# Gathering the tokens of an expert in one-pass products, and turning the SwiGLU rows 128 at a time

## The reference, cut to what matters

```python
x = x + gt1 * mix
h = rmsnorm(x, norm_ffn) * (1.0 + sc2) + sh2
# one group of 4 by argmax, its top 2 of 8 experts, softmax weights: comb
for grp in range(4):
    hg  = einsum('nd,edf->enf', h, w_exp_gate[grp])     # 8 experts, 2048 -> 512
    hu  = einsum('nd,edf->enf', h, w_exp_up[grp])
    hid = silu(hg) * hu * wgt.T[:, :, None]
    out = out + einsum('enf,efd->nd', hid, w_exp_down[grp])
```

## Time and profile before

| | us |
|---|---|
| median of 3 runs | 1876.94 |
| the profiled execution | 1875.18 |
| its span | 1873.5 |
| PE busy, weight loads busy | 1771.7, 1267.9 |
| DVE, ACT, POOL busy | 714.0, 471.0, 212.7 |

### The profile page before, as it was taken

One profiled execution on the slowest core, in us unless ns is written; L12 is line 12 of the kernel. 1 busy time (PEld: TensorE's weight loads), 2 busy tenths in 40 slices (PEclk: granted clock), 3 DMA queues, 4 the chain that ended last, 5 costly groups with the idle time before them and its releaser, 6 DMA issues.

```text
span 1873.5 us, 37855 instructions
## 1 busy us (share of the span) xinstructions
PE 1771.7 (95%) x16527; PEld 1267.9 (68%) x16527; DVE 714.0 (38%) x1523; ACT 471.0 (25%) x842; POOL 212.7 (11%) x295
## 2 busy tenths in 40 slices
PE   5689999999988989999899999999999999999997
PEld 2168779988856666899666656666566665666656
DVE  1145564455673554643222333222322223222234
ACT  3044333444621211344211111111111111111114
POOL 1000000021038780333000000000000000000000
PEclk8889999999999999899999999999999999999997
DMA  9989884674388779342699999999999999999992
GB/s 365 419 304 335 299 309 135 202 254 152 135 310 349 297 301 372 109 146 91 281 431 428 434 431 432 432 430 434 429 434 430 432 432 430 435 428 434 431 432 78
DMA packets 111124, 629.71 MB, mean 336 GB/s; under 512 B 8932, under 2 KB 76956, under 8 KB 81823
## 3 DMA queue, kind: packets, MB, share of 16 engines
q1 hardware_dynamic: 105150, 608.45, 80.1%
q0 software_dynamic: 5120, 17.44, 2.8%
q10 hardware_dynamic: 754, 2.33, 0.4%
HBM read 618.65 MB, written 9.56 MB: 335 GB/s over the span
## 4 chain that ended last, share of the span: by engine, by line
PE 43%; DMA 13%; DVE 1%; issue 0%; ACT 0%; POOL 0%; POOLq 0%; DVEq 0%; ACTq 0%
PE pb L2712 18%; DMA ring<-in_w_exp_up 13%; PE pb L2691 7%; PE pb L2725 6%; PE pb L2701 2%; PE pb L2702 2%; PE pb L2069 2%; PE pb L2070 2%; PE pb L2071 1%; PE pb L2734 1%; PE pb L2607 0%; PE pb L2744 0%; PE pb L2741 0%; PE pb L2614 0%; PE pb L2742 0%
## 5 line engine op out<-in xcount | busy, mean ns | idle before, releaser
L2712 PE MATMUL pb<-ring,pj 128*64 128x256 f32 x4096 | 466.0, 381 | 5.8 <-DMA ring<-in_w_exp_up 5.8
L2712 PEld LDWEIGHTS pb<-ring,pj 128*64 128x64 f32 x4096 | 285.9, 137 | 170.6 <-DMA ring<-in_w_exp_up 19.9
L2069 PE MATMUL pb<-ht_parts,ring_parts 128*128 128x264 f32 x1056 | 309.2, 293 | 7.1 <-DVE ring_parts L1324 6.2
L2070 PE MATMUL pb<-ring_parts 128*128 128x264 f32 x1056 | 301.9, 286 | 0.0
L2071 PE MATMUL pb<-ring_parts 128*128 128x264 f32 x1056 | 301.4, 285 | 0.0
L2725 PE MATMUL pb<-ring,pj 128*64 128x512 f32 x1024 | 226.0, 594 | 0.0
L2069 PEld LDWEIGHTS pb<-ht_parts,ring_parts 128*128 128x128 f32 x1056 | 201.6, 191 | 24.1 <-issue 16.0
L1864 DVE TENSOR_TENSOR pj_parts<-pb,pj_parts 64x512 fp32r<-64x512 f32 x128 | 88.2, 689 | 311.3 <-ACT pj_parts L1186 309.3
L2070 PEld LDWEIGHTS pb<-ring_parts 128*128 128x128 f32 x1056 | 201.8, 191 | 0.0
L2071 PEld LDWEIGHTS pb<-ring_parts 128*128 128x128 f32 x1056 | 200.7, 190 | 0.0
L1324 DVE TENSOR_TENSOR ring_parts<-ring,ring_parts 128x2048 fp32r<-128x2048 f32 x50 | 114.6, 2291 | 173.6 <-ACT ring_parts L790 173.5
(11 more groups left out here) (470 smaller groups left out, 1962.4 us busy)
## 6 DMA issues: line engine op xcount, KB each, us to landing
ring<-in_w_exp_gate SPq DMA_DIRECT2D x32, 4096.0 KB, 17.7
ring<-in_w_exp_up SPq DMA_DIRECT2D x32, 4096.0 KB, 15.5
ring<-in_w_exp_down SPq DMA_DIRECT2D x32, 4096.0 KB, 17.1
ring<-in_w_ada SPq DMA_DIRECT2D x32, 2048.0 KB, 15.2
ring<-in_w_in SPq DMA_DIRECT2D x24, 2048.0 KB, 9.3
pj<-in_w_ada SPq DMA_DIRECT2D x32, 1024.0 KB, 7.8
ring<-in_w_ada_final SPq DMA_DIRECT2D x16, 2048.0 KB, 13.0
ring<-in_w_out SPq DMA_DIRECT2D x8, 2048.0 KB, 8.5
```

The lines of the kernel that those rows point to most:

```text
L2069: pe.matmul(out, hi[:, k, :], ht_lo[:, k, :], start=(k == 0), stop=False)
L2070: pe.matmul(out, lo[:, k, :], ht_hi[:, k, :], start=False, stop=False)
L2712: last = pe.matmul(pb[bank][SLOT * h:SLOT * h + SLOT, e * 256:(e + 1) * 256], xg[:, k, SLOT * e:SLOT * e + SLOT], w[:, k, h * 256:(h + 1) ...
```

## The change

Each token block is written once in two parts: `h_hi`, the scaled token rounded to float32r, and `h_lo`, the remainder. The gather multiplies both with `disp`, now also float32r (0 and 1). The two parts take 4 MB together: `h_lo` takes the place of `h_tok`, and `h_hi` lies in five pieces in memory of three tensors that are free by then (`lm`, `ct`, `ada_row`) and in the free end of `ht`. ACT writes the five pieces of `h_hi`, two ahead of the first exponential, two behind it, one behind the second; POOL scales `h_tok` in place and subtracts `h_hi`, piece by piece (10 instructions). The first gather waits for two remainders, the third for all five. `moe_turn` becomes 4 transposes of all 128 rows, and ACT takes each of them out in two copies.

```diff
+        h_lo = pj_r[:, at[0]:at[0] + TC * D].rearrange("p (c k r) -> p c k r", c=TC, r=P)
         h_tok = room(TC * D).rearrange("p (c k r) -> p c k r", c=TC, r=P)
+        H_HI = [[(range(0, 8), lm_r[:]), (range(8, 12), ct_r[:]), (range(12, KD), ada_r[:])],
+                [(range(0, 8), ht_r[:, D + P:D + P + 1024]), (range(8, KD), ht_r[:, D + P + 1024:2 * D + P])]]
+        H_ORDER = [(0, 0), (1, 0), (0, 1), (0, 2), (1, 1)]
...
+            pool.wait_ge(*once("rs_mid"))
+            pool.wait_ge(S("h2t_evac"), KD)
+            for i, (c, part) in enumerate(H_ORDER):
+                ks, mem = H_HI[c][part]
+                at = slice(ks[0], ks[-1] + 1)
+                pool.wait_ge(S("h_norm"), i + 1)
+                pool.tensor_scalar(h_tok[:, c, at, :], h_tok[:, c, at, :], ms_tok[:, c:c + 1], None, ALU.mult)                    .then_inc(S("h_scaled"), 1)
+                pool.wait_ge(S("h_scaled"), i + 1)
+                pool.tensor_tensor(h_lo[:, c, at, :], h_tok[:, c, at, :], mem.bitcast(F32).rearrange("p (k r) -> p k r", r=P),
+                                   ALU.subtract).then_inc(S("h_low_out"), 1)
...
-            tokens_out(0)
+            act.wait_ge(*once("rs_mid"))
+            act.wait_ge(S("h2t_evac"), KD)
+            for c, part in H_ORDER[0:2]:
+                tokens_out(c, part)
             act.wait_ge(*once("rt_d1"))
             act.activation(g_exp, g_exp, ACT.Exp).then_inc(once("rt_e1")[0], 1)
+            for c, part in H_ORDER[2:4]:
+                tokens_out(c, part)
             act.wait_ge(*once("rt_d2"))
             act.activation(e2, e2, ACT.Exp).then_inc(once("rt_e2")[0], 1)
-            tokens_out(1)
+            tokens_out(*H_ORDER[4])
...
-                    act.copy(hid_t[:, e], pb[6][:, e * 256:(e + 1) * 256].rearrange("p (c s) -> p c s", s=SLOT))\
-                        .then_inc(S("m_ht"), 1)
+                    turned = pb[6][0:SLOT, :].rearrange("p (c h s) -> p h c s", h=2, s=SLOT)
+                    act.copy(hid_t[0:SLOT, e], turned[:, 0])
+                    act.copy(hid_t[SLOT:P, e], turned[:, 1]).then_inc(S("m_ht"), 1)
...
                 for j in range(4):
+                    k = 4 * b + j
                     for c in range(TC):
-                        last = pe.matmul(pb[bank][:, j * P:(j + 1) * P], h_tok[:, c, 4 * b + j, :], disp[:, c, :],
-                                         start=(c == 0), stop=(c == TC - 1))
+                        pe.matmul(pb[bank][:, j * P:(j + 1) * P], h_lo[:, c, k, :], disp_r[:, c, :], start=(c == 0), stop=False)
+                        last = pe.matmul(pb[bank][:, j * P:(j + 1) * P], h_hi(c, k), disp_r[:, c, :], start=False, stop=(c == TC - 1))
...
                 for c in range(4):
-                    for h in range(2):
-                        r = slice(SLOT * h, SLOT * h + SLOT)
-                        last = pe.matmul(pb[6][r, e * 256 + c * SLOT:e * 256 + (c + 1) * SLOT], sg_in_rows[r, e, c, :],
-                                         ident[r, r], start=True, stop=True)
+                    last = pe.transpose(pb[6][0:SLOT, c * P:(c + 1) * P], sg_in_rows[:, e, c, :], ident[:])
...
                     pe.wait_ge(S("sh_evac"), 4)
+                    pe.wait_ge(S("h_low_out"), 5)
                     moe_gather(2, FIRST_BANKS[2])
...
-                    pe.wait_ge(S("h_norm"), TC)
+                    pe.wait_ge(S("h_low_out"), 2)
                     moe_gather(0, FIRST_BANKS[0])
```

More of the change, by code:

```diff
@@ L103, in sb @@
             return ctx.enter_context(nc.sbuf_tensor(name, [rows, cols], dt))
-        sizes = (("ring", (MOE_SLOTS - 1) * RING + KD * NT), ("ht", KD * NT), ("g2", 1024), ("pj", NTILE * NT))
+        sizes = (("ring", (MOE_SLOTS - 1) * RING + KD * NT), ("ht", KD * NT), ("g2", 1024), ("pj", NTILE * NT),
+                 ("lm", 8 * P), ("ct", KD * CPAD), ("ada_row", BANK))
         with ExitStack() as parts:
-            ring_r, ht_r, g2_r, pj_r = (parts.enter_context(nc.sbuf_tensor(f"{name}_parts", [P, cols], F32R))
+            ring_r, ht_r, g2_r, pj_r, lm_r, ct_r, ada_r = (parts.enter_context(nc.sbuf_tensor(f"{name}_parts", [P, cols], F32R))
                                   for name, cols in sizes)
-        ring, ht_flat, g2, pj_flat = (sb(name, cols) for name, cols in sizes)
+        ring, ht_flat, g2, pj_flat, lm_flat, ct_flat, ada_row = (sb(name, cols) for name, cols in sizes)
         ta = ring[:, MIX_SLOTS * RING:MOE_SLOTS * RING]
@@ L122, in hymba_layer @@
         bones = sb("bones", P)
-        ct = sb("ct", KD * CPAD)[:].rearrange("p (k n) -> p k n", n=CPAD)
-        lm = sb("lm", 8 * P)[:].rearrange("p (l n) -> p l n", n=P)
+        ct = ct_flat[:].rearrange("p (k n) -> p k n", n=CPAD)
+        lm = lm_flat[:].rearrange("p (l n) -> p l n", n=P)
         mstrict = sb("mstrict", P)
@@ L132, in hymba_layer @@
         om_ka = sb("om_ka", 8)
-        ada_row = sb("ada_row", BANK)
         rstd = sb("rstd", NT)[:]
@@ L240, in hymba_layer, with h_hi @@
         most_f, most = room(1), room(1).bitcast(I32)
+        h_lo = pj_r[:, at[0]:at[0] + TC * D].rearrange("p (c k r) -> p c k r", c=TC, r=P)
         h_tok = room(TC * D).rearrange("p (c k r) -> p c k r", c=TC, r=P)
+        H_HI = [[(range(0, 8), lm_r[:]), (range(8, 12), ct_r[:]), (range(12, KD), ada_r[:])],
+                [(range(0, 8), ht_r[:, D + P:D + P + 1024]), (range(8, KD), ht_r[:, D + P + 1024:2 * D + P])]]
+        H_ORDER = [(0, 0), (1, 0), (0, 1), (0, 2), (1, 1)]
+        def h_hi(c, k):
+            at, = [mem[:, (k - ks[0]) * P:(k - ks[0] + 1) * P] for ks, mem in H_HI[c] if k in ks]
+            return at
         xg = room(KD * P).rearrange("p (k s) -> p k s", s=P)
@@ L247, in hymba_layer @@
         hid_t = room(FF).rearrange("p (e c s) -> p e c s", e=2, s=SLOT)
+        disp_r = pj_r[:, at[0]:at[0] + TC * P].rearrange("p (c s) -> p c s", c=TC)
         disp = room(TC * P).rearrange("p (c s) -> p c s", c=TC)
@@ L1132, in _, with tokens_out @@
             mid_out(KD - 1)
[L1134 to L1138, removed]
-            tokens_out(0)
+            def tokens_out(c, part):
+                ks, mem = H_HI[c][part]
+                act.activation(mem.rearrange("p (k r) -> p k r", r=P), h_tok[:, c, ks[0]:ks[-1] + 1, :], ACT.Identity,
+                               scale=ms_tok[:, c:c + 1]).then_inc(S("h_norm"), 1)
+            act.wait_ge(*once("rs_mid"))
+            act.wait_ge(S("h2t_evac"), KD)
+            for c, part in H_ORDER[0:2]:
+                tokens_out(c, part)
             act.wait_ge(*once("rt_d1"))
             act.activation(g_exp, g_exp, ACT.Exp).then_inc(once("rt_e1")[0], 1)
+            for c, part in H_ORDER[2:4]:
+                tokens_out(c, part)
             act.wait_ge(*once("rt_d2"))
             act.activation(e2, e2, ACT.Exp).then_inc(once("rt_e2")[0], 1)
-            tokens_out(1)
+            tokens_out(*H_ORDER[4])
             def sh_out(b):
@@ L1831, in moe_dispatch @@
                     for c in range(TC):
-                        last = dve.tensor_scalar(disp[:, c, q * SLOT:(q + 1) * SLOT], slot_no[:, 0, :],
+                        last = dve.tensor_scalar(disp_r[:, c, q * SLOT:(q + 1) * SLOT], slot_no[:, 0, :],
                                                  slots[:, c, bass.ds(t * 2 + q, 1)], None, ALU.is_equal)
@@ L2740, in moe_places @@
                 for c in range(TC):
-                    pe.matmul(pb[6][:, 0:2], disp[:, c, :], comb[:, c, bass.ds(i * 2, 2)], start=(c == 0), stop=False)
+                    pe.matmul(pb[6][:, 0:2], disp_r[:, c, :].bitcast(F32), comb[:, c, bass.ds(i * 2, 2)], start=(c == 0), stop=False)
                 pe.matmul(pb[6][:, 0:2], own_slot, comb[0:NS, TC, bass.ds(i * 2, 2)], start=False, stop=True)
                 for c in range(TC):
-                    last = pe.transpose(pb[7][:, c * P:(c + 1) * P], disp[:, c, :], ident[:])
+                    last = pe.transpose(pb[7][:, c * P:(c + 1) * P], disp_r[:, c, :].bitcast(F32), ident[:])
                 last.then_inc(S("m_wt"), 1)
```

## The result

The changed kernel takes 1889.97 us (median of 4 runs, 1886.39 to 1892.24) against 1877.63 us for the kernel before beside it: ratio 1.006, 95% interval 1.0045 to 1.0075. Worked out from the ratio that is +11.3 us, 8.4 to 14.1; the two medians themselves lie 12.3 us apart. The forecast was 1883 us. With 1889.97 us the result also lies beyond the 1886.3 us from which the prediction calls a time "slower", to which it gave a chance of 0.36.

The account below looks back on a forecast made before the run. DMA bounds the expert loop, so only head and tail count: head +8.0 - 0.4, tail -0.4 - 0.6, +6.6 us on 1875.18 is 1881.8; with 1.8 us to the runs' median, 1883. Range about 1873 to 1893.

Parts of the forecast that it names:

- The loop hides it: Expert loop: DMA sets the pair's 58.3 us, so a shorter PE part, busy some 56.5, changes nothing.
- Gather, 111 ns a product, set by the weight load: Gather parts: loading 128 stationary columns sets the pace, so a part takes 1.78 us in place of 1.88.
- -0.4 us in the tail: Tail after the last "up 1": four gather parts, each 0.1 us shorter.
- Turn, -0.6 us: Tail: 4 transposes take 0.43 to 0.5 us in place of 1.09; hidden in the loop.
- The lock of POOL and DVE, 7 to 10, taken as 8: Head, routing chain: POOL's instructions hold off DVE's two-input ones, so `routed` comes 7 to 10 us late.
- Nothing later is delayed in its own right: Head behind routing: PE, ACT and SP only wait behind `routed`; DMA's empty stretch grows by as much.
- -0.4 in the head from the gathers: Head, first gathers: four parts, each 0.1 us shorter.
- Rival A: Routing chain: POOL holds DVE with whole instructions, +11.5 to +15 in the head, 1887 to 1891 us; chance 0.22.
- B: Head: small DVE instructions slip by or scaling doesn't lock, 0 to 5 us, 1875.5 to 1880.5; chance 0.15.
- C: Gathers: 128 columns, not the weight load, pace the product; about 1876 us, without delay 1868; chance 0.10.
- D: Gathers: one-pass product takes 236 ns at 128 columns, PE becomes the bound, about 1990 us; chance 0.08.

Follow-up runs that it names:

- five-fold low products: Changed kernel with the first low product of each tile issued five times in place of once; 1982.36 us, ratio 1.0552.
- without POOL: Changed kernel with POOL's ten instructions left out, the low product multiplying the rounded part again; 1880.59 us, ratio 1.0024.
- pace measurement: Changed kernel with seven series of 24 float32r products, of varied stationary and moving columns, ahead of the counting; 1900.74 us, series included.
- layout alone: Kernel before, with only lm, ct and ada_row allocated as in the changed kernel; 1877.46 us, ratio 1.001.
- late POOL: Changed kernel, but POOL starts its third piece only when the first dispatch is done; 1886.93 us, ratio 1.0062.
- fillers: Changed kernel plus float32 products on the identity in PE's idle time, 28 ahead of the counting and 15 ahead of the first gather; 1880.4 us, ratio 1.0023.
- DVE remainder: Changed kernel with the remainder made by DVE in eight instructions of 512 columns, POOL idle; 1882.02 us, ratio 1.0026.
- DVE remainder, fillers: Changed kernel with DVE making the remainder, plus 3 float32 products ahead of the counting and 7 ahead of the first gather; 1879.03 us, ratio 1.0013.
- all cuts: Kernel before with its float32 gather, the new turn, 3 + 7 filler products, and the last pair's gather parts cut to one product; 1872.97 us, ratio 0.9966.
- peel: Kernel before with only the last pair written out, its four gather parts being one product of 64 columns each; 1872.25 us, ratio 0.9975.
- turn alone: Kernel before with only moe_turn changed to 4 transposes and two ACT copies; 1874.99 us, ratio 0.9988.

## Why the prediction was right and wrong

The measured +11.3 us lies inside the range, and the sign is right; the forecast of +6.6 was 4.7 us low. By its own steps:

- **The loop hides it: right.** 58.28 us a pair, PE busy 56.48 (forecast 56.5). The five-fold low products confirm 1.8 us of slack.
- **Gather, 111 ns a product, set by the weight load: right in the pace** (112 ns by itself, 108 in place in the loop, 64 moving columns no quicker than 128). The -0.4 us in the tail was not seen: the two gathers of 32 gave 0.05 us each (3.77 to 3.72; 3.57 beside the same turn to 3.52). I had set a computed 1.78 us against a measured 1.88; in the chain the new gather goes at 3.72 / 32 = 116 ns.
- **Turn, -0.6 us: mis-sized**, 0.85 us with the gather behind it. The tail came out at -0.9 for a forecast -1.0, by two errors that met. The 106 ns of a transpose were a slip: sixteen starts have fifteen intervals, so the earlier trace rows give (1.95 - 0.275) / 15 = 112 ns, and four in the chain took 0.44 to 0.46 us, within the stated 0.43 to 0.5.
- **The lock of POOL and DVE, 7 to 10, taken as 8: right as a mechanism, mis-sized at 6.2 us.** Without POOL it is 0.05 us (10.71 against 10.66). The single holds were right: a subtraction was priced at 2.2 us and adds 2.02 and 2.10, a scaling was priced at 0.86 us (1024 columns) and 0.43 (512) and adds 0.87 and 0.45. What failed is the window between holds. It was taken as 0.2 to 0.3 us, since POOL's scaling was priced like a copy, with the whole sequence at 14 us. The scaling of 1024 columns took 2.86 us, and from the first POOL instruction to the end of the last it is 21.8 us (901.69 to 923.47). (Spans on POOL are rough, but the start of the next instruction says the same: 2.94 us behind the scaling, 2.32 behind the subtraction.) After that first stretch of a scaling DVE ran freely: at 903.51, in the midst of it, L1806 takes 0.18 us. So routing was done after five holds, 6.3 us, and not after the 8 us that were reckoned from nearly all of them. Subtracting holds for its whole length. The Trainium skill ("SBUF — State Buffer", section "SBUF: two separate sides") has the lock held for the whole instruction; the trace agrees for the subtraction and not for the scaling.
- **"Nothing later is delayed in its own right": this step failed.** It holds the other 6.6 us of the head (12.74 less 6.18). Not all of them are the lock's, since the head of the kernel without POOL is still 3.3 us longer than before. Because POOL was still at work when routing was done, the dispatch was held off as well, one-input instructions though they are: +2.2 us (0.74 again when POOL waits). The same section of the Trainium skill's "SBUF — State Buffer" also puts DVE instructions in a two-port performance mode under the lock; the 2.58 us would agree with that, but no run shows which mode these are in. Counting ran at half clock: +1.1. From first gather to load: +3.4, at a clock of 0.73 in place of 0.92. I had read the first gather's 3.53 us before as a price of the lower clock, and then took for granted that the clock would recover behind it as before.
- **-0.4 in the head from the gathers: wrong sign**, since it is part of that same +3.4 us. At the full clock a late gather of the head takes 1.99 us in place of 2.05; at the half clock the second one takes 3.64 in place of 2.02.
- **Rival A** (the lock costs more) gave the closest time, 1887 to 1891, but not for its reason: routing was delayed by less than forecast, not more. That its range holds the result, while the forecast's own sum is 4.7 us low, is luck: what it left out was the clock and the dispatch. **B** fell: small instructions don't slip by, and the scaling does lock, if only for the first third of its length. **C** and **D** fell to the pace measurement. The Trainium skill's fast weight load for types other than FP32 ("TensorE: Matmul & The Clock Gate", section on weight-path perf modes) isn't seen for float32r, whose 112 ns are the 110 to 111 of the earlier trace rows.

As a test of the marks, here are the three distances from t0 to the last down product added up, against the runs' ratio (us against before, 95% in brackets):

| kernel | by the marks | by the runs |
|---|---|---|
| changed | +11.6 | +11.3 (8.4 to 14.1) |
| layout alone | +0.2 | +1.9 (-0.4 to 4.1) |
| without POOL | +2.4 | +4.5 (1.3 to 7.7) |
| late POOL | +13.2 | +11.6 (6.9 to 16.1) |
| fillers | +8.2 | +4.3 (2.1 to 6.8) |
| DVE remainder | +7.0 | +4.9 (2.1 to 7.9) |
| DVE remainder, fillers | +4.5 | +2.4 (-0.2 to 4.9) |
| all cuts | -6.8 | -6.4 (-8.8 to -4.1) |
| peel | -5.4 | -4.7 (-7.1 to -2.3) |
| turn alone | -0.95 | -2.3 (-4.5 to 0.2) |

One, the fillers on the changed kernel, lies outside. Its profiled execution took 1885.89 us, 5.5 above the median of its runs, so its marks may not be those of a usual one; why it was slow isn't shown.

**Open.** Why the clock stays low behind one-pass gathers isn't settled. Shown is that it does with POOL idle, and that float32 gathers in their place let it rise after the first one (0.89 over the stretch in the layout kernel). 43 float32 products ahead brought the clock up for the gathers in the changed kernel, though it fell again behind them, while 10 didn't in the one with DVE's remainder. Against the gathers as the only cause stands that the kernels without POOL and with DVE's remainder give PE the same instructions, and the clock comes back 9.9 us apart, each in one profile. Which property of the products decides wasn't separated, and neither the place of the first gather after a pause nor plain scatter from one execution to the next is excluded.

## What to carry to other kernels

An empty engine isn't free: before work is put on POOL, list the DVE instructions that run in its whole length, including those behind the first one that it delays, one-input ones too. When PE's work is made lighter in a stretch that begins at the half clock, price the stretch at either level, since the clock may come back later than before. And in a DMA-bound loop look at what the last turn does for no one: cutting that was worth 5 us, more than anything on the way.

## What the runs showed of the hardware

- POOL's tensor_scalar with a per-partition scalar took 2.86 us for 1024 columns and 1.57 for 512, longer than its two-input subtraction (2.34 and 1.26 to 1.45) and near three times the 1.03 us of a copy of 1024 (on 16 partitions).
- A DVE instruction with two inputs that began with it took 1.05 us (1024) or 0.63 us (512) in place of 0.18, after which DVE ran freely beside it; the subtraction held for its whole length (2.20 and 2.28 us).
- DVE's dispatch, four instructions of one tensor input and 64 columns, took 2.58 us beside POOL and 0.74 alone.
- PE fell to the half clock while it ran one-pass products of 32 moving columns without a pause, and rose again behind one-pass products of 128 moving columns on 64 and 32 stationary ones (0.50 in those series, 1.00 in the one of 256 that followed).
